# Neighbourhood attention: bias and minimum in one instruction over all 512 keys, two pairs of heads scored before the last value slab

## What is computed

```python
def neighbourhood_attention(q, k, v, k_ctx, v_ctx, rpb):
    # for each grid row r; kh = 4 rows here, 16 columns around the query's
    bias = jnp.take(bias_col, rel_row, axis=1).transpose(0, 2, 1, 3)
    s_nb = jnp.einsum('bchd,brcwhd->bhcrw', q_r, k_win) * scale + bias[None]
    s_cx = jnp.einsum('bchd,bkhd->bhck', q_r, k_ctx) * scale
    p = jax.nn.softmax(jnp.concatenate([s_nb, s_cx], axis=-1), axis=-1)
    return einsum(p_nb, v_win) + einsum(p_cx, v_ctx)
```

## Time and profile before

| what | value |
|---|---|
| median of 3 runs | 2055.31 us (2055.27 to 2055.6) |
| the profiled execution | 2058.96 us, of which the span is 2057.1 us |
| PE busy | 2029.4 us, 99% of the span |
| DVE busy | 1371.3 us, 67% |
| ACT busy | 754.6 us, 37% |
| granted TensorE clock | 1.00 over the span |
| from the first scores to the out projection | 1763.38 us to 1830.27 us of the span |

### The profile page before, as it was taken

The page is one execution under the profiler, slowest core; times in us unless marked ns, Lnnn a source line. Parts: engine busy times, 40 slices in busy tenths (PEclk is TensorE's granted clock), DMA queues, the critical chain, the costliest instruction groups (busy, mean ns, idle before and its releaser), DMA issues. The chain is left out here.

```text
span 2057.1 us, 30253 instructions
## 1 busy us (share of the span) xinstructions
PE 2029.4 (99%) x12728; PEld 1762.6 (86%) x12728; DVE 1371.3 (67%) x2147; ACT 754.6 (37%) x936; POOL 154.1 (7%) x138
## 2 busy tenths in 40 slices
PE   9999999999999999999999999999999999999998
PEld 8979979888888988688888888888888899779998
DVE  6966975776785667657876775655455465567555
ACT  4464465222213544435222222521212242565333
POOL 0410500000002000020000003000000210010001
PEclk9999999999999999999999999999999999999999
DMA  6653654554543210223454543332532343114552
GB/s 242 227 173 140 242 182 156 188 198 166 204 159 120 114 44 9 105 82 132 180 191 174 194 173 124 123 141 93 196 133 98 118 165 141 55 61 152 188 174 103
DMA packets 68768, 301.39 MB, mean 147 GB/s; under 512 B 6176, under 2 KB 23200, under 8 KB 48672
## 3 DMA queue, kind: packets, MB, share of 16 engines
q1 hardware_dynamic: 65920, 290.06, 39.0%
q10 hardware_dynamic: 2720, 9.51, 1.3%
HBM read 298.50 MB, written 1.05 MB: 146 GB/s over the span
## 5 line engine op out<-in xcount | busy, mean ns | idle before, releaser
L482 PE MATMUL PS<-xh,wh 128*128 128x512 f32 (+1 forms) x3676 | 1000.8, 347 | 2.5 <-DVE wh L398 1.0
L482 PEld LDWEIGHTS PS<-xh,wh 128*128 128x128 f32 x3676 | 659.0, 188 | 91.9 <-issue 1.7
L482 PE MATMUL PS<-xl,wh 128*128 128x512 f32 (+1 forms) x2086 | 706.4, 339 | 0.0
L394 ACT ACTIVATE wh<-raw 128x2048 fp32r<-128x2048 f32 (+4 forms) x221 | 377.6, 1710 | 301.3 <-PE PS L482 227.6
L398 DVE TENSOR_TENSOR wh<-raw,wh 128x2048 fp32r<-128x2048 f32 (+3 forms) x183 | 376.2, 2056 | 101.8 <-ACT wh L394 101.4
L482 PEld LDWEIGHTS PS<-xl,wh 128*128 128x128 f32 x2086 | 391.9, 188 | 43.9
L482 PE MATMUL PS<-HH,wh 128*128 128x512 f32 (+1 forms) x1276 | 347.8, 359 | 0.1
L1349 DVE CUSTOM_DVE_ANT_0 NRM<-SQ,CBR 128x1024 f32<-128x1024 f32 x240 | 284.0, 1221 | 5.8
L1270 ACT ACTIVATE SI<-PS 128x512 f32<-128x512 f32 (+1 forms) x88 | 47.9, 544 | 584.1 <-PE PS L482 569.7
L482 PEld LDWEIGHTS PS<-HH,wh 128*128 128x128 f32 x1276 | 227.3, 188 | 37.2 <-DVE wh L398 0.9
L482 PE MATMUL PS<-HL,wh 128*128 128x512 f32 (+1 forms) x638 | 228.6, 358 | 0.0
(11 more groups left out here) (416 smaller groups left out, 2376.9 us busy)
## 6 DMA issues: line engine op xcount, KB each, us to landing
raw<-ffi_dram SPq DMA_DIRECT2D x88, 1024.0 KB, 4.9
SQ<-adat_dram SPq DMA_DIRECT2D x120, 512.0 KB, 3.4
raw<-ffo_dram SPq DMA_DIRECT2D x64, 704.0 KB, 4.2
raw<-layer_dram SPq DMA_DIRECT2D x36, 1024.0 KB, 5.0
lent<-layer_dram SPq DMA_DIRECT2D x14, 1024.0 KB, 7.3
raw<-odd_dram SPq DMA_DIRECT2D x12, 1024.0 KB, 4.8
raw<-even_dram SPq DMA_DIRECT2D x9, 1024.0 KB, 4.8
raw<-eout_dram SPq DMA_DIRECT2D x4, 1024.0 KB, 4.9
```

The costliest lines, as they stand in the source:

```text
L394: act.activation(high(i)[:, 0:n], raw[:, i.slot, 0:n], ACT.Copy).then_inc(hi_done, 1)
L482: m = pe.matmul(out, w[rows, o:o + P], x, start=n == 0 and j == 0, stop=n == len(tiles) - 1 and j == 2)
```

## The change

- M becomes one `tensor_tensor_reduce` over all 512 keys, from a constant start. The bias of the context keys is zero: `bias_and_nothing` makes a view of two rows of 256 columns, the first in the head's own bias, the second in a block of zeros behind all the heads. To have each head's six rows in one piece, `RPB` holds 6 instead of 7 rows a head, and four of zeros, which DVE sets.
- S(1) is moved ahead of the last value slab, beside S(0). The banks become 4, 5, 6, 7 for pairs 0 and 1, and then 0 to 3 in turn. S(2) and S(3) wait for the copies of the two last value slabs, and the first O waits for the exponentials of pair 1, whose bank it takes.
- M(0) to M(3) and X(0) to X(3) stand in slab 11, and N(0) to N(3) ahead of DVE's turns.
- From turn 1 on, DVE's order is M(2w+2), N(2w), M(2w+3), N(2w+1), where N(2w) stood ahead of M(2w+2). (Turn 1 has no N, since they are done.)
- PE's order in a turn stays.

```diff
-        od = phase([("nmask", [P, 64]), ("RPB", [P, 16, 7, 64]), ...
+        od = phase([("nmask", [P, 64]), ("RPB", [P, 16 * 6 + 4, 64]), ...
         def score_bank(v):
-            return 4 + v if v < 2 else (v - 2) % 4
+            return 4 + v if v < 4 else v % 4
+        def bias_and_nothing(h, blk):
+            at, end = (6 * h + 2 - 2 * blk) * 64, 16 * 6 * 64
+            rows = od["RPB"][:, 0:4, :]
+            return bass.AP(rows.tensor, rows.offset + at, [list(rows.ap[0]), [end - at, 2], [1, T]])
         def pe_scores(pe, w):
-            if w >= 3:
+            if w >= 4:
                 pe.wait_ge(on["n_exp"], 2 * w - 2)
...
             def output(w):
                 pe.wait_ge(on["n_copy"], 2 * w + 2)
+                if w == 0:
+                    pe.wait_ge(on["n_exp"], 4)
...
-            pe.wait_ge(drained[1 - last.par], (last.d - 1) // 2 + 1)
-            pe_scores(pe, 1)
             for w in range(NA_PAIRS):
                 turn(w)
-                if w == 0:
-                    pe.wait_ge(drained[last.par], last.d // 2 + 1)
                 if w + 2 < NA_PAIRS:
+                    if w < 2:
+                        pe.wait_ge(drained[w], (last.d - (last.d - w) % 2) // 2 + 1)
                     pe_scores(pe, w + 2)
...
         def dve_maxima(dve, ch, v):
-                least, nm = tiny[:, 12 + v % 4:13 + v % 4], tiny[:, v % 4:v % 4 + 1]
-                ch.after(dve.tensor_reduce(least, PS[:, score_bank(v), T:2 * T], AX, ALU.min))
-                o = PS[:, score_bank(v), 0:T]
-                dve.tensor_tensor_reduce(out=o, in0=o, in1=od["RPB"][:, h, 3 - 2 * blk:7 - 2 * blk, :].rearrange("p r c -> p (r c)"),
-                                         scale=1.0, scalar=least, op0=ALU.add, op1=ALU.min, accum_out=nm).then_inc(on["n_soft"], 1)
+                nm = tiny[:, v % 4:v % 4 + 1]
+                o = PS[:, score_bank(v), :].rearrange("p (b n) -> p b n", b=2)
+                dve.tensor_tensor_reduce(out=o, in0=o, in1=bias_and_nothing(h, blk), scale=1.0, scalar=-TAKEN, op0=ALU.add, op1=ALU.min,
+                                         accum_out=nm).then_inc(on["n_soft"], 1)
...
-            for w in range(NA_PAIRS):
+            for v in range(4):
+                normal(v)
+            for w in range(1, NA_PAIRS):
                 for e in range(2):
-                    normal(2 * w + e)
                     if w + 1 < NA_PAIRS:
                         dve_maxima(dve, ch, 2 * w + 2 + e)
+                    if w > 1:
+                        normal(2 * w + e)
...
-            act.dma_start(od["RPB"][:, :, :, :], a["rpb"]).then_inc(on["c3_in"], 16)
+            act.dma_start(od["RPB"][:, 0:96, :], a["rpb"].rearrange("p h d c -> p (h d) c")).then_inc(on["c3_in"], 16)
...
                 if k == 11:
-                    act_exp(act, 0)
-                    act_exp(act, 1)
+                    for v in range(4):
+                        act_exp(act, v)
...
                     if k == 11:
                         pe_scores(pe, 0)
+                        pe_scores(pe, 1)
...
                 if k == 11:
-                    for v in range(2):
+                    for v in range(4):
                         dve_maxima(dve, ch, v)
...
-                    rp = od["RPB"][:, :, :, :].rearrange("p h d c -> p (h d) c")
-                    dve.tensor_tensor(rp, bc(od["nmask"][:, :], 112), rp, ALU.subtract).then_inc(on["qkv_ready"], 1)
+                    dve.memset(od["RPB"][:, 96:100, :], 0.0)
+                    rp = od["RPB"][:, 0:96, :]
+                    dve.tensor_tensor(rp, bc(od["nmask"][:, :], 96), rp, ALU.subtract).then_inc(on["qkv_ready"], 1)
...
-    out["rpb"] = np.concatenate([rp[0:HD, :, 1:8], rp[HD:, :, 0:7]])
+    out["rpb"] = np.concatenate([rp[0:HD, :, 2:8], rp[HD:, :, 1:7]])
```

More of the change, by code:

```diff
@@ L338, in build @@
                     ("QR", [P, 2, 2 * T]), ("KN", [P, 4, 2 * T]), ("VM", [P, 4, 512])])
-        od = phase([("nmask", [P, 64]), ("RPB", [P, 16, 7, 64]), ("NQ", [P, 8, T]), ("NK", [P, 8, 2 * T]),
+        od = phase([("nmask", [P, 64]), ("RPB", [P, 16 * 6 + 4, 64]), ("NQ", [P, 8, T]), ("NK", [P, 8, 2 * T]),
                     ("NV", [P, 4, 1024]), ("NP", [P, 4, 512]), ("NPT", [P, 4, 512])])
@@ L2043, in act_pairs @@
             for w in range(NA_PAIRS):
[L2044 to L2049, removed]
+                for e in range(2):
+                    if w and w + 1 < NA_PAIRS:
+                        act_exp(act, 2 * w + 2 + e)
+                    copy(2 * w + e)
                 if w and w % 2 == 0:
```

## The result

The changed kernel is slower: 2066.86 us median of six runs (2064.72 to 2068.38) against 2055.78 for the kernel before (six runs, 2055.27 to 2056.18). The medians lie 11.1 us apart; the ratio is 1.0051, 95% interval 1.0040 to 1.0062, that is some 10.5 us. The forecast was +9.3 us. Between the two profiled executions the span grew from 2057.1 to 2066.2 us, 9.1 us.

The account below looks back on a forecast made before the run. A ring of waits between PE and DVE, 3.36 us a turn, not one engine, was taken to bound the heads. -1.65 + 11 x 0.95 + 0.54 = +9.3 us on 2055.3 gave 2064.6 us, range 2059.0 to 2067.5.

Parts of the forecast that it names:

- The ring, 3.09 + 2m: Heads, S to next S through DVE's two M and two N: 4.31 us a turn, 0.95 more than 3.36.
- The old order's 2.49 + m: Heads, turn if N(2w) did not stand behind the wait for S: one M in it, 3.10 us.
- PE's own work: Heads, PE's scores, outputs and eight transposes with the change to S: 3.09 us a turn.
- m = 0.61: DVE, time from the merged M's start to the next instruction's: 0.61 us, where two instructions took 0.87.
- The start: From S(0) past the last value slab to S(4): S(4) comes 1.65 us ahead of before.
- The end: From S(15) to the out projection: 8.25 us, 0.54 more than before.
- At nothing: Bias minus mask, memset, bias transfer, weights and moved tiles, outside the turns: no time taken for them.
- The sum: Whole change: -1.65 + 11 x 0.95 + 0.54 = +9.3 us, from a median of 2055.3 to 2064.6.
- The bounds: Forecast's limits: 2059.6 for m = 0.41 and 2066.5 for m = 0.68; with a microsecond for misreadings, 2059.0 to 2067.5.
- Rival 1: Heads: the order costs nothing, PE's 3.09 us sets the turn, -6.5 us, 2048.8; chance 6%.
- Rival 2: Heads: PE's clock drops to 1.2 GHz as PE waits more, 16 us on top, 2081; chance 3%.
- Rival 3: Heads: turns stay at 3.36 us and the head start stands alone, -1.65 + 0.5, 2054.2; chance 4%.

Follow-up runs that it names:

- e3: The changed kernel with M as the two old instructions; order, banks and early scores as changed: ratio 1.0067, stage 83.03 us.
- e5: The changed kernel with the start of M's minimum taken from an SBUF column instead of a constant: stage 78.04 us, one run.
- e2: The kernel before with only the merged M (and the rows and zeros it needs): ratio 0.9978, stage 62.95 us.
- e1: The changed kernel with DVE's old order back, N(2w) ahead of M(2w+2): ratio 0.9971, stage 61.08 us.
- e4: The changed kernel with S(w+2) put ahead of T(2w) and T(2w+1) on PE, DVE's new order kept: ratio 0.9973, stage 61.37 us.
- r2_after_again: The changed kernel run once more, nothing altered, for a second profile: stage 76.43 us, span 2070.4 us.

## Why the prediction was right

The forecast was 2064.6 us. Sign and mechanism are as measured, and the median of 2066.86 is 2.3 us above it. Of these 2.3 us the stage explains 0.2 (9.55 against 9.3) and the median of the kernel before 0.5 (2055.78 against the 2055.3 that the forecast started from). The rest, some 1.5 us, lies outside the stage, and no run shows that it comes from the change. Step by step:

- **The ring, 3.09 + 2m.** Measured 1.16 + 0.61 + 0.20 + 0.40 + 0.61 + 0.20 + 0.54 + 0.59 = 4.31, each term as it was put down. e3 and e5 give it at two more values of m: 4.82 for 0.87 (4.83 by the sum), and 4.44 for the 0.68 and 0.67 that e5's two M take to the next start (4.44 by the sum). The old order's 2.49 + m = 3.10 stands in e2's first turn, 3.11; in e1 and in e2's later turns PE's own work, forecast at 3.09, sets the same 3.11. The names in the prediction's reading of the old turn are off: what follows S(4) there is M(8), N(7) and T(7), and not M(10), N(9) and T(9). The times are of the right rows, so the sum stands.
- **m = 0.61.** Right, and for the reason given: 701 ns long and 0.61 to the next start, and e5 prices the column at 55 ns, where 60 to 70 had been taken off.
- **The start.** Forecast 1.65 us ahead at S(4), measured 1.53. Two readings were off and nearly cancel. S(0) and S(1) back to back took 1.92 us (1765.81 to 1767.73) and not 2.10; but the last slab took 11.31 us (1767.73 to 1779.04) and not 11.10, and the first T with its change to S 1.07 and not 1.01. That they cancel is luck.
- **The end.** From S(15) to the out projection 8.26 us; forecast 8.25.
- **At nothing.** The bias minus mask took 6.50 us and PE did not stop for it (43.40 of 43.40). "lo" fell into DVE's wait. ACT had room. All right.
- **The sum** for the stage, +9.3, against +9.55 measured (-1.53 + 10.53 + 0.55). Split by the experiments: the merging -3.94 (e2 against before), the early scores -1.87 (e1 against e2), the order +15.36 (after against e1). In the forecast the first two never stood by themselves, since the ring swallowed them; they are what the changed kernel gives away. The bounds hold small slips: by the prediction's own ring the end is 0.68 and not 0.66 for m = 0.68, and 0.14 and not 0.3 for m = 0.41, and a microsecond below 2059.6 is 2058.6 and not 2059.0. Together they would put the lower bound at 2058.4 and leave the upper one.
- **Rival 1**, without the order's cost, was put at -6.5. e1 is that case and gave -5.81 in the stage: the turn was 3.11 and not 3.09, the first turn after S(3) 3.22 (1782.52 to 1785.74), and the end 7.30 and not 7.0 (1819.92 to 1827.22).
- **Rival 2**, the clock, did not come. One flaw in how I put it: I held 3.09 of 4.31, 72%, against busy shares of the view by stretches, which counts a matmul to its modelled end. In that view the stretch had 79%, above the 76% that had already been seen at full clock. The case for this rival was weaker than it was made. e3 went further: with turns of 4.82 us the clock was 1.00 there too, with PE busy for 9.53 of 13.00 us (1784.30 to 1797.30). The Trainium skill, "TensorE: Matmul & The Clock Gate", Part 4, says that transposes don't count as busy in the same way; these traces, 1.00 in the heads after and in e3, show no sign that it mattered here.
- **Rival 3** fell with the turns.

One instruction in place of two took 0.26 us off each head's M, some 0.06 of it by the column (e5). For 28 heads 0.26 is 7.3 us of DVE's time, and the stage in e2 got 3.94 shorter: DVE's work as a whole did not set the pace, only the part of it in the ring, and the old ring holds one M of a turn's two. The Trainium skill, "VectorE: DVE Perf Modes", in the section on the TRN2 errata, says that operations which read from SBUF pay a fixed extra latency per instruction, so that one large one is cheaper than many small ones. M reads its scores from PSUM and only the bias from SBUF; the saving in e2 agrees with the rule in kind, and no run here separates the two memories.

## What to carry to other kernels

Where engines work through fixed orders, write down for each cross-engine wait what is queued behind it and whether the thing waited for is itself behind that queue; the sum round that ring is the turn, and busy shares don't show it. "Issued a turn ahead" is only true if the producer's order puts it ahead of what the consumer must first deliver: here either N before M on the consumer or S before T on the producer is enough, and having neither cost 15 us (15.36 against e1, 15.07 against e4). A merged instruction is worth its saving only on the ring, and there as often as it occurs in it. The version with the merging, the early scores and the old order (e1) beats both kernels, by 0.29% against before (95% interval 0.17% to 0.41%).

## What was not expected of the hardware

The rate at which PE takes 256-column matmuls has two values, and which of them a stage gets can differ between executions of the same program. The slabs of the last feed-forward are alike, and an activation of ACT marks each. In the first profile of after:

```profile
1982.30 0.39 ACT L1270 ACTIVATE SI<-PS 128x256 f32<-128x256 f32 x1 [3.25 <-PE PS L482]
1987.74 0.39 ACT L1270 ACTIVATE SI<-PS 128x256 f32<-128x256 f32 x1 [3.25 <-PE PS L482]
```

and in the second profile of the same kernel (r2_after_again):

```profile
1984.72 0.38 ACT L1270 ACTIVATE SI<-PS 128x256 f32<-128x256 f32 x1 [3.46 <-PE PS L482]
1990.38 0.38 ACT L1270 ACTIVATE SI<-PS 128x256 f32<-128x256 f32 x1 [3.46 <-PE PS L482]
```

That is 5.44 us a slab or 5.66, 4% more, for the same 48 matmuls, 113 or 118 ns each. The kernel before showed 5.65 in its second half of this stage in both of its profiles, and 5.44 in several slabs of the first half. The granted clock does not tell the two apart: over some twelve slabs of the second half it was 1.00 both in before (68.11 us) and in after (65.72 us), with nearly the same number of matmuls:

```profile
1960.32:2028.43 68.11, 68.04 (x578) 67.83 (x577) 40.67 (x48) 26.10 (x25) 1.47 (x2) 1.00 0.46 160
```

```profile
1971.84:2037.56 65.72, 65.50 (x577) 65.30 (x577) 40.56 (x48) 26.15 (x25) 1.48 (x2) 1.00 0.48 169
```

The slabs with 512 columns took 10.88 us in every profile.

In the last value slab the same two rates follow the kernel and not the execution: from S(0) to S(2), with 96 such matmuls between, all seven profiles with the early scores in which T(0) and T(1) stand between the slab and S(2) took 14.30 us, and the slab's 11.31 us in after are 118 ns a matmul; the three profiles with S(1) behind the slab took 12.15 us from S(0) to S(1). This is where the 11.31 us came from that the prediction had at 11.10.

Between the first and the second profile of the changed kernel, the slabs of the last feed-forward took 3.6 us more, of 4.2 in the whole span. So the two rates are most of that difference, and they are a reason why a change of a few microseconds is safer read from its stage than from the total (before ran from 2055.23 to 2061.81 us in the fourteen executions beside e1 to e4). What sets the rate was not found.
